# GpSimd makes the low half of a weight chunk in four instructions instead of one

## The chip, the cores and the metric

The kernel runs on one core of a Trainium2 chip. The metric is device time in microseconds (us) from the first to the last instruction of an execution and what lies around it, lower is better. A core has a matrix engine (TensorE, PE in the profile, with PEld for its weight loads), VectorE (DVE), ScalarE (ACT), GpSimd (POOL) and SyncE (SP), which here only issues transfers. Each engine works through its own queue in order; they wait for one another by semaphores.

## The reference

Two layers (gated linear attention; sparse attention with an indexer that picks the best keys), each with layer norm and a gated embedding, and then a second block with five groups of mixers. All of it is in float32, and most of the time goes into products of a 512-token activation with large weights:

```python
def gla_mixer(x, w_in, w_a2, b_a, gn_g, w_out):
    h = x @ w_in                                   # 1024 x 6160
    ...
    return (o.astype(x.dtype) * jax.nn.silu(z)) @ w_out
...
for i in range(DEPTH):
    ...                                            # y = gla_mixer(...) or dsa_mixer(...)
    x = layer_norm(ALPHA * x + y, ln_g[i], ln_b[i])
    x = x + (p[i] @ ple_w[i]) * jax.nn.sigmoid(x @ ple_gate_w[i])
```

The kernel makes such a product from three faster ones: a weight w is split into a rounded high half and the rest, `low = w - high`, the activation likewise, and high x high, high x low and low x high are added up in PSUM (`split_product`, L211).

## The kernel before, in words

Weights come in chunks of 256 columns by 1024 rows: on the chip a tile of 128 partitions x 8 k-tiles x 256 columns, 2048 float32 values a partition, 1 MB. Three rings of RING = 2 slots hold them: `w_ring` (as loaded), `w_high` and `w_low`. A chunk goes through four engines in order:

- `load_chunks` (SyncE): waits until the low half of the chunk that held the slot before is made (`w_low_made`), then issues the transfer into `w_ring`.
- `split_high` (ScalarE, L184): waits for the landing and for TensorE's release of the chunk two before, then copies `w_ring` to `w_high`, rounding it.
- `split_low` (GpSimd, L193): waits for `w_high_made` and subtracts: `w_low = w_ring - w_high`. It counts `w_low_made`.
- `chunk` (TensorE): waits for `w_low_made` and uses both halves, 48 or 96 matrix instructions over some 11 us. The matrix instructions of all products are recorded at L209.

The first chunk of all is split apart from this, in two halves (L451), and is not touched by the change. The very last one is 2 k-tiles of 1024 columns. Two chunks are narrow, 72 and 80 columns a k-tile. The two `mem_w_kv` chunks are not split and do not pass here.

Which phases the prediction speaks of:

- `phase_post`, once behind each layer: the output projection, then layer norm token tile by token tile. `layer_norm(j)` on VectorE is a chain of small steps around two instructions of 1024 columns, L1173 (inputs `x` and `gain`) and L1178 (inputs `x` and `shift`), with a square root on ScalarE between them (L1074, `rstd_x`). TensorE meanwhile multiplies an embedding (`w_ple`), waits for the first gate chunk, uses it for token tile 0, and then turns the `x` of token tile 2 (L879, waits for L1178).
- `phase_dsa`, the sparse attention: rotations on VectorE (L1547 to L1552), and from about 662 us the top-k search: L1602 and L1603 sixteen times over a tile, then L1604 (a subtraction with two inputs) and L1605 (a scalar operation).
- `phase_project`, the second block's projections: `norm_heads` on VectorE is L2002 and L2005 for each token tile, with two inputs in SBUF each; behind two of them stands L2022, which makes `a_tok`, for which TensorE waits.
- `phase_rwkv`, the last phase: chains of two-input instructions (L3172, L3174, L3175, `bt` at L3181), beside three GpSimd subtractions of the same kind at L3149 that the change leaves alone.

Of the kernel before, what the change touches and what calls it, by code (L numbers as in the profile page):

```python
# [7 lines left out]
F32 = mybir.dt.float32  # L8
# [16 lines left out]
RING = 2  # L25
# [51 lines left out]
class Program:  # L77
# [109 lines left out]
    def split_low(self, pool, upto=None):  # L187

        while self.lows < self.highs and (upto is None or self.splits[self.lows] < upto):
            i, n = self.lows, self.splits[self.lows]  # L190
            _, k, cols, _, _ = self.chunks[n]
            pool.wait_ge(self.w_high_made, i + 1)
            self.nc.gpsimd.tensor_tensor(self.slot(self.w_low, i % RING, k, cols), self.slot(self.w_ring, n % RING, k, cols),  # L193
                                         self.slot(self.w_high, i % RING, k, cols).bitcast(F32), ALU.subtract).then_inc(self.w_low_made, 1)
            self.lows += 1

    def chunk(self, pe, n):
# [3277 lines left out]
```

## Time and profile before

| | |
|---|---|
| median of 3 runs | 1610.26 us (1609.72 to 1610.45) |
| profiled execution | 1610.07 us, its span 1608.3 us |
| TensorE busy | 1510.5 us, 94% |
| VectorE busy | 678.1 us, 42% |
| ScalarE busy | 528.4 us, 33% |
| GpSimd busy | 549.9 us, 34%, 216 instructions |
| L193, GpSimd, all low halves | 414.1 us busy, 91 instructions, 803.4 us idle before them |
| mean granted TensorE clock | 0.971 |

Times in the rows are counted from the span's start. Busy time is the union of an engine's instructions. An instruction of VectorE or GpSimd that is issued and can't begin shows as a long one, so what looks like work may be waiting. A row of the timeline ends, in brackets, with the engine's idle time before it and what ended it. The granted clock is 1.00 at the higher of TensorE's two levels (2.4 GHz) and 0.50 at the lower (1.2 GHz).

### The profile page before, as it was taken

To read this page: it belongs to the slowest core of one execution; us is meant where nothing else is said; L and a number is where in the kernel's file an instruction comes from. 1 tells how busy PE (TensorE), PEld (TensorE's weight loads), DVE (VectorE), ACT (ScalarE), POOL (GpSimd) and SP (SyncE) were. 2 spreads that over 40 slices of the span, in tenths; PEclk is the share of its full clock that TensorE was granted. 3 is DMA by queue.
4 is the path that set the end of the run, shared out by engine and by line. 5 is a ranking of instruction groups with operands and counts; after the bars stand their busy time and mean duration, and the time that the engine had idled before them with its cause. 6 is when DMAs were issued, how large, how long until landed. Compare 5 with 4: busy or idle time off the path is not lost. (4 is left out here: it accounts for less than half of the span.)

```text
span 1608.3 us, 23500 instructions
## 1 busy us (share of the span) xinstructions
PE 1510.5 (94%) x9997; PEld 1312.5 (82%) x9997; DVE 678.1 (42%) x1356; ACT 528.4 (33%) x862; POOL 549.9 (34%) x216
## 2 busy tenths in 40 slices
PE   7999999999999999988999999999989997858998
PEld 7898875998997977766787899889879875748897
DVE  7032540222144273695545214441252135688424
ACT  3444225232223223333444222343342244421211
POOL 6333420333332248642643233224242411412121
PEclk9999999999999999998999999999999999978999
DMA  5223220223312332220111422243332200020111
GB/s 163 90 68 102 82 75 5 63 96 139 137 62 71 112 100 84 76 82 27 53 53 34 160 83 79 67 153 89 105 93 65 79 26 1 0 79 1 54 53 53
DMA packets 113751, 121.21 MB, mean 75 GB/s; under 512 B 12530, under 2 KB 107614, under 8 KB 113391
## 3 DMA queue, kind: packets, MB, share of 16 engines
q1 hardware_dynamic: 110096, 113.77, 22.2%
q10 hardware_dynamic: 3550, 5.94, 1.0%
q8 instruction: 79, 1.29, 0.3%
q14 instruction: 26, 0.21, 0.0%
HBM read 113.41 MB, written 6.29 MB: 74 GB/s over the span
## 5 line engine op out<-in xcount | busy, mean ns | idle before, releaser
L193 POOL TENSOR_TENSOR w_low<-w_ring,w_high 128x2048 fp32r<-128x2048 f32 (+1 forms) x91 | 414.1, 4550 | 803.4 <-ACT w_high L184 803.0
L209 PE MATMUL ps<-w_high,xT_high 128*128 128x256 f32 (+1 forms) x1056 | 305.1, 289 | 9.3 <-POOL w_low L451 4.4
L209 PE MATMUL ps<-w_high,xT_low 128*128 128x256 f32 (+1 forms) x1056 | 299.1, 283 | 0.0
L209 PE MATMUL ps<-w_low,xT_high 128*128 128x256 f32 (+1 forms) x1056 | 299.0, 283 | 0.0
L184 ACT ACTIVATE w_high<-w_ring 128x2048 fp32r<-128x2048 f32 (+1 forms) x91 | 171.5, 1885 | 316.5 <-PE ps L209 311.0
L209 PE MATMUL ps<-xT_high,w_high 128*128 128x512 f32 (+1 forms) x600 | 242.4, 404 | 2.8 <-POOL w_low L193 1.8
L209 PE MATMUL ps<-xT_high,w_low 128*128 128x512 f32 (+1 forms) x600 | 238.7, 398 | 0.0
L209 PE MATMUL ps<-xT_low,w_high 128*128 128x512 f32 (+1 forms) x600 | 237.6, 396 | 0.0
L209 PEld LDWEIGHTS ps<-w_high,xT_high 128*128 128x128 f32 x1056 | 202.8, 192 | 16.6 <-issue 6.4
L209 PEld LDWEIGHTS ps<-w_low,xT_high 128*128 128x128 f32 x1056 | 202.7, 192 | 1.7 <-issue 1.7
L209 PEld LDWEIGHTS ps<-w_high,xT_low 128*128 128x128 f32 x1056 | 202.3, 192 | 0.0
L209 PE MATMUL ps<-w_high,gT_high 128*128 128x256 f32 x512 | 146.2, 286 | 3.9 <-DVE gT_low L288 3.9
L209 PE MATMUL ps<-w_high,gT_low 128*128 128x256 f32 x512 | 145.6, 284 | 0.0
L209 PE MATMUL ps<-w_low,gT_high 128*128 128x256 f32 x512 | 145.5, 284 | 0.0
L209 PEld LDWEIGHTS ps<-xT_high,w_high 128*128 128x128 f32 (+1 forms) x600 | 112.9, 188 | 32.4 <-issue 2.9
L209 PEld LDWEIGHTS ps<-xT_high,w_low 128*128 128x128 f32 (+1 forms) x600 | 112.5, 188 | 28.4
L209 PEld LDWEIGHTS ps<-xT_low,w_high 128*128 128x128 f32 (+1 forms) x600 | 112.9, 188 | 26.3
L209 PEld LDWEIGHTS ps<-w_high,gT_high 128*128 128x128 f32 x512 | 99.0, 193 | 4.4 <-DVE gT_low L288 4.4
L209 PEld LDWEIGHTS ps<-w_low,gT_high 128*128 128x128 f32 x512 | 99.0, 193 | 0.0
L209 PEld LDWEIGHTS ps<-w_high,gT_low 128*128 128x128 f32 x512 | 98.9, 193 | 0.0
L209 PE MATMUL ps<-dsa_kT,mix_a 128*128 128x128 f32 (+3 forms) x128 | 42.8, 464 | 12.1 <-DVE peak L1615 12.1
L1155 DVE SCALAR_TENSOR_TENSOR x<-x,ps 128x512 f32<-128x512 f32 x16 | 10.9, 684 | 102.6 <-PE ps L209 102.6
(504 smaller groups left out, 2287.1 us busy)
## 6 DMA issues: line engine op xcount, KB each, us to landing
w_ring<-in_gla_w_in_dram SPq DMA_DIRECT2D x24, 1024.0 KB, 5.4
w_ring<-in_dsa_w_in_dram SPq DMA_DIRECT2D x19, 1024.0 KB, 5.1
w_ring<-in_w_in_dram SPq DMA_DIRECT2D x18, 1024.0 KB, 5.2
w_ring<-in_gla_w_out_dram SPq DMA_DIRECT2D x8, 1024.0 KB, 4.9
w_ring<-in_ple_gate_w_dram SPq DMA_DIRECT2D x8, 1024.0 KB, 5.1
w_ring<-in_dsa_w_out_dram SPq DMA_DIRECT2D x8, 1024.0 KB, 5.1
x_scratch<-x SPq DMA_DIRECT2D x4, 1024.0 KB, 6.3
w_ring<-in_w_out_dram SPq DMA_DIRECT2D x4, 768.0 KB, 4.8
```

The lines of the kernel that those rows point to most:

```text
L184: self.nc.scalar.activation(self.slot(self.w_high, i % RING, k, cols), self.slot(self.w_ring, n % RING, k, cols), ACT.Copy).then_inc(self. ...
L193: self.nc.gpsimd.tensor_tensor(self.slot(self.w_low, i % RING, k, cols), self.slot(self.w_ring, n % RING, k, cols), self.slot(self.w_high, ...
L209: return self.nc.tensor.matmul(out, lhs, rhs, start=first, stop=last, skip_group_check=not check)
L1155: nc.vector.scalar_tensor_tensor(out=r[:, j, cols], in0=x[:, j, cols], scalar=ALPHA, in1=ps[:, i, :], op0=ALU.mult, op1=ALU.add).then_inc( ...
```

## The change

`split_low` cuts the k-tiles of a chunk into steps of a quarter (2 of 8) and issues one subtraction for each. Only the last one counts the semaphore `w_low_made`. So who waits for a chunk still waits for all of it.

```diff
             pool.wait_ge(self.w_high_made, i + 1)
-            self.nc.gpsimd.tensor_tensor(self.slot(self.w_low, i % RING, k, cols), self.slot(self.w_ring, n % RING, k, cols),
-                                         self.slot(self.w_high, i % RING, k, cols).bitcast(F32), ALU.subtract).then_inc(self.w_low_made, 1)
+            low, whole, high = (self.slot(w, m % RING, k, cols) for w, m in ((self.w_low, i), (self.w_ring, n), (self.w_high, i)))
+            step = -(-k // 4)
+            for a in range(0, k, step):
+                part = slice(a, min(a + step, k))
+                ins = self.nc.gpsimd.tensor_tensor(low[:, part], whole[:, part], high[:, part].bitcast(F32), ALU.subtract)
+            ins.then_inc(self.w_low_made, 1)
             self.lows += 1
```

In GpSimd's queue before, from the first layer's chunks (24 in a row) over the norm stage (12, behind L1244) to the first rotated heads of the sparse attention:

```order
L862 UNCONDITIONAL_BRANCH
L193 TENSOR_TENSOR w_low<-w_ring,w_high 128x2048 x24
L1244 UNCONDITIONAL_BRANCH
L193 TENSOR_TENSOR w_low<-w_ring,w_high 128x2048 x12
L1664 UNCONDITIONAL_BRANCH
L193 TENSOR_TENSOR w_low<-w_ring,w_high 128x2048
L193 TENSOR_TENSOR w_low<-w_ring,w_high 128x8x72
L193 TENSOR_TENSOR w_low<-w_ring,w_high 128x2048 x2
L1667 TENSOR_TENSOR mix_a<-mix_a,head_cos 32x512
```

The same place of the changed kernel, whose lines stand four further down:

```order
L866 UNCONDITIONAL_BRANCH
L197 TENSOR_TENSOR w_low<-w_ring,w_high 128x512 x96
L1248 UNCONDITIONAL_BRANCH
L197 TENSOR_TENSOR w_low<-w_ring,w_high 128x512 x48
L1668 UNCONDITIONAL_BRANCH
L197 TENSOR_TENSOR w_low<-w_ring,w_high 128x512 x4
L197 TENSOR_TENSOR w_low<-w_ring,w_high 128x2x72 x4
L197 TENSOR_TENSOR w_low<-w_ring,w_high 128x512 x8
L1671 TENSOR_TENSOR mix_a<-mix_a,head_cos 32x512
```

Nothing changes its place; each instruction of a chunk has become four, and the queues of the other engines hold what they held.

## Rows read from the trace of the kernel before

**Rows 1.** Waits of TensorE: who waited for whom, us in total, times, longest:

```profile
PE ps L209 <- DVE peak L1615: 12.1, 4, 11.1
...
PE ps L209 <- POOL w_low L193: 5.2, 3, 1.8
...
PE ps L1867 <- DVE a_tok L2022: 4.7, 1, 4.7
...
PE ps L879 <- DVE x L1178: 3.8, 2, 1.9
```

**Rows 2.** GpSimd by shape: count, busy us, mean ns, idle before:

```profile
L193 POOL TENSOR_TENSOR w_low<-w_ring,w_high 128x2048 fp32r<-128x2048 f32 x89 | 411.1, 4619 | 792.6 <-ACT w_high L184 792.1 <-POOL level L465 0.3
```

**Rows 3.** Timeline (start, us, engine, line), GpSimd behind a low half:

```profile
613.28 1.29 POOL L1667 TENSOR_TENSOR mix_a<-mix_a,head_cos 32x512 f32<-32x512 f32 x1
...
614.53 1.29 POOL L1668 TENSOR_TENSOR rot<-rot,head_sin 32x512 f32<-32x512 f32 x1
```

**Rows 4.** Timeline of GpSimd, then of VectorE, last phase:

```profile
1452.26 3.81 POOL L3149 TENSOR_TENSOR mix_low<-mixT,mix_high 128x1536 fp32r<-128x1536 f32 x1 [20.11 <-DVE branch_room L3175]
...
1456.02 3.88 POOL L3149 TENSOR_TENSOR mix_low<-mixT,mix_high 128x1536 fp32r<-128x1536 f32 x1
...
1459.86 2.81 POOL L3149 TENSOR_TENSOR mix_low<-mixT,mix_high 128x1024 fp32r<-128x1024 f32 x1
...
1452.69 3.91 DVE L3181 TENSOR_TENSOR bt<-LT,levelT 128x512 f32<-128x512 f32 x1
```

**Rows 5.** Timeline of GpSimd, first layer-norm stage:

```profile
475.43 4.52 POOL L193 TENSOR_TENSOR w_low<-w_ring,w_high 128x2048 fp32r<-128x2048 f32 x1 [16.89 <-ACT w_high L184]
```

**Rows 6.** Timeline of VectorE, first layer-norm stage:

```profile
476.06 4.98 DVE L1173 SCALAR_TENSOR_TENSOR x<-x,moments,gain 128x1024 f32<-128x1024 f32 x1
...
481.14 5.42 DVE L1178 SCALAR_TENSOR_TENSOR x<-x,rstd_x,shift 128x1024 f32<-128x1024 f32 x1
```

**Rows 7.** Timeline of ScalarE, first layer-norm stage:

```profile
478.85 0.19 ACT L1074 ACTIVATE rstd_x<-rstd_x 128x1 f32<-128x1 f32 x1
```

**Rows 8.** Timeline of TensorE, first layer-norm stage:

```profile
480.00 0.38 PE L209 MATMUL ps<-w_high,xT_high 128*128 128x256 f32 x1 [1.68 <-POOL w_low L193]
...
486.70 0.30 PE L879 MATMUL ps<-ident,x 128*128 128x128 f32 x1 [1.90 <-DVE x L1178]
```

**Rows 9.** Stretches of TensorE: length, busy (instructions), granted clock, DMA share, GB/s:

```profile
480.80:484.10 3.30, 3.30 (x23) 1.00 0.88 287
593.40:596.70 3.30, 3.30 (x10) 0.50 0.93 310
1204.40:1211.10 6.70, 5.40 (x26) 0.50 0.47 153
```

**Rows 10.** Timeline of GpSimd, then VectorE, then TensorE, chunk at 587:

```profile
587.41 4.75 POOL L193 TENSOR_TENSOR w_low<-w_ring,w_high 128x2048 fp32r<-128x2048 f32 x1 [11.01 <-ACT w_high L184]
...
587.76 4.94 DVE L1552 TENSOR_TENSOR prob<-prob,dsa_gated 128x512 f32<-128x512 f32 x1
...
592.21 0.50 PE L209 MATMUL ps<-xT_high,w_high 128*128 128x512 f32 x1 [1.83 <-POOL w_low L193]
```

**Rows 11.** Timeline of GpSimd, then VectorE, top-k search:

```profile
674.81 4.64 POOL L193 TENSOR_TENSOR w_low<-w_ring,w_high 128x2048 fp32r<-128x2048 f32 x1 [2.71 <-ACT w_high L184]
...
678.39 1.35 DVE L1604 TENSOR_TENSOR left<-left,prob 128x256 f32<-128x256 f32 x1
...
679.77 0.29 DVE L1605 TENSOR_SCALAR left<-left 128x256 f32<-128x256 f32 x1
```

**Rows 12.** Timeline of GpSimd, then VectorE, head norms:

```profile
1198.55 4.57 POOL L193 TENSOR_TENSOR w_low<-w_ring,w_high 128x2048 fp32r<-128x2048 f32 x1 [6.56 <-ACT w_high L184]
...
1199.71 4.49 DVE L2002 TENSOR_TENSOR heads<-heads,head_ss 128x1024 f32<-128x1024 f32 x1
...
1205.47 0.17 DVE L2022 TENSOR_TENSOR a_tok<-gates,cum 128x16 f32<-128x16 f32 x1
```

**Rows 13.** Timeline of VectorE, last phase:

```profile
1429.88 2.81 DVE L3172 TENSOR_TENSOR branch_room<-LT,levelT 128x512 f32<-128x512 f32 x1
```

## The prediction

> **What bounds the kernel now.** I read the page's busy shares first: TensorE works 94% of the span, GpSimd 34%, so GpSimd as such is no bound. Then TensorE's waits [rows 1]: of its idle time only 5.2 us, in three pieces, ends with a low half made at L193. All other chunks are ready before TensorE asks for them. But the same list names waits on VectorE that belong to this change: two on `x` (L1178, 3.8 us), one on `a_tok` (L2022, 4.7 us) and an 11.1 us one on `peak` (L1615) behind VectorE's top-k search. In the timeline some VectorE instructions with two SBUF inputs last exactly until a GpSimd instruction ends and then their own length: 4.98 us for x at L1173 [rows 6], whose 1024 columns take the 1.08 us that are left behind the low half's end at 479.95 [rows 5, 6]. So VectorE and GpSimd exclude each other there, instruction by instruction. The change cuts the piece that VectorE waits for; it also lets VectorE in between the pieces of a chunk that TensorE waits for.
>
> **One chunk by itself.** A low half of 2048 columns takes 4.62 us (89 of them) [rows 2]. A GpSimd two-input instruction of 512 columns takes 1.29 us, and the next starts 1.25 us after it [rows 3]. Four of them: 3 x 1.25 + 1.29 = 5.04, that is +0.43 us a chunk. Bounds: +0.54 if nothing overlaps (4 x 1.29 - 4.62), +0.1 if the pieces lose nothing but their own start, from rows 4: of the low halves at L3149 the first ends 3.28 us after the port was given back (1452.78 to 1456.06) with 1536 columns, the last 2.22 us after it (1460.45 to 1462.67) with 1024, so 2.07 ns a column and 0.10 us fixed; 4 x (0.10 + 1.06) = 4.64. I take 0.43, the row of the same length. In all, 90 chunks become four instructions and one becomes two. 91 x 0.43 = 39 us more of GpSimd, nearly all beside TensorE's work: rows 1 have three waits on L193 and no more; by the timeline a steady chunk is used 3.6 us or more after its end, and the tightest that don't wait have 0.9 and 1.7 us. In the attention layer GpSimd also has the rotations of the heads in its queue and is busy from 608.7 to 646 without a pause, so four chunks' additions pile up there to 1.7 us; its chunks have over 6 us to spare in that stretch. SyncE's next load waits for the last piece too, 0.43 us later, which ScalarE hides by waiting for TensorE's release anyway.
>
> The Trainium skill ("GPSIMD Engine Reference", section 3.1) gives 2.6 cycles an element at 1.2 GHz and 4497 ns for 2048 columns; that leaves some 60 ns of fixed cost, and by that estimate four pieces would cost +0.18 us a chunk. The row of 512 columns speaks for more; the sum would be 0.8 us smaller by the page.
>
> **Who gets in between.** Three GpSimd instructions stand back to back with VectorE's bt (L3181) queued [rows 4]: the first GpSimd one ends at 1456.06, the second is issued at 1456.02, and yet VectorE's ends at 1456.61 (1452.69 + 3.91, the chain's 4.44 us for two) and the second GpSimd one at 1459.90, late by VectorE's 0.55 us. They take turns. So with four pieces, a two-input VectorE instruction waits for at most one piece, and each one that comes costs the chunk its own length. A piece right behind VectorE takes 0.10 + 1.06 = 1.16 us.
>
> The Trainium skill ("SBUF — State Buffer", section "SBUF: two separate sides") says that the pair of ports is an exclusive lock held for the whole instruction. The trace agrees (4.98 us for x). By that rule alone the cut would only help VectorE; what it does to the chunk is the turns of rows 4.
>
> **The two layer-norm stages** (475 and 996, alike to 0.02 us). Now: low half 475.43 to 479.95, TensorE waits 1.68 until 480.00 [rows 5, 8]; x of L1178 is held by the next low half until 486.56, TensorE waits 1.90 until 486.70. After: piece 1 ends 476.72; L1173 (asked at 476.06) runs to 477.80; piece 2 to 478.96; piece 3 to about 480.20, since L1178 needs ScalarE's rstd_x, made 479.04 [rows 7], and comes too late for that turn; L1178 runs to 481.28; piece 4 to 482.44. TensorE starts at 482.48, not 480.00: +2.48. From there its next 4.80 us of work (480.00 to 484.80) are as before, so it comes to x at 487.2 and x has long been there: the 1.90 goes. Net +2.48 - 1.90 = +0.6, less some 0.1 of overlap: **+0.5 each, +1.0**. Bounds for one: 0.2 (pieces at their cheapest) to 0.9.
>
> Two waits of under 2 us become one of 1.68 + 2.48 = 4.16 us. The granted clock [rows 9] is 1.00 after the idle 1.68 (480.8 to 484.1) but 0.50, the lower level of 1.2 GHz, after the idle 1.83 at 592.21 and for 6.7 us after the idle 4.71 at 1205.70. So I expect a stretch at the lower level in both stages. Work in it takes twice its time: 3.3 us busy in the row at 593.4 is a loss of 1.65, 5.4 us at 1204.4 a loss of 2.7; part of the stretch can fall into the wait itself. I take 1.5 each, **+3.0**; bounds 0 and 2.7 each.
>
> **Chunk at 587.41** [rows 10]. One VectorE instruction (L1552, 0.55 us net) is in it. Pieces: 588.70; L1552 to 589.25; 590.41; 591.65; 592.90. TensorE starts 592.95 instead of 592.21: **+0.7**, and the clock has fallen there already. Bounds 0.3 to 1.0.
>
> **Top-k search.** VectorE is the bound from 661.7 to 728.8. There L1604 waits for a low half (1.35 us instead of the 0.4 that 256 columns take) [rows 11]. With pieces: low half from 674.81, the third ends 678.60, L1604 runs to 678.88; the fourth, waiting, takes its turn until 680.04; L1605, in SBUF on both sides too, waits for it and ends about 680.2 instead of 680.06. The stall has moved by one instruction. A second round, at 700, goes alike. **+0.2** for both; if L1605 doesn't need the port, -1.9.
>
> **Head norms** [rows 12]. L2002, L2005 and L2022 follow one another on VectorE and TensorE waits for a_tok. Now: the low half ends 1203.12, L2002 1204.20, L2005 (1024 columns too) some 1.1 later, a_tok 1205.64. After: piece 1 ends 1199.84, L2002 1200.92, piece 2 1202.08, L2005 1203.16, piece 3 1204.32, a_tok 1204.36: TensorE starts at 1204.4, not 1205.70, **-1.3**, with the last piece behind it where nobody waits (that chunk has 14 us to spare). The idle time falls from 4.71 to 3.4, so I take the shorter of the stretches at the lower level for the longer one, 2.7 - 1.65, **-1.0**. Bounds -2.6 and -0.9 together.
>
> **Last phase.** At 1429.88 L3172 waits 2.1 us for a low half [rows 13] on the chain that ends last, but L3174 and L3175, with two SBUF inputs each, come right behind it and let the remaining pieces in. They end where they did, **+0.1**. The other stalls of VectorE (v_tok at L856, gate at L1221, the rotations before 587) end before anyone waits for them.
>
> Sum: 1.0 + 3.0 + 0.7 + 0.2 - 2.3 + 0.1 = **+2.7 us** on the profiled execution's 1610.07 (span 1608.3 and 1.8 around it), which is 0.19 under the median of 1610.26: **1612.8 us**. A measurement of this kernel can tell about 0.2%, 3.2 us, from no change.
>
> **The rivals.**
> - *The clock costs more.* If the three stretches are as long as the one at 1204.4 and the head norms keep theirs: 2 x (0.9 + 2.7) + 1.0 + 0.4 - 1.3 + 0.1 = +7.4, 1617.5. For it: an idle 4.71 did this once. Against: that stretch held transposes and a part of the wait.
> - *The clock stays up* in both norm stages, as it did after 1.68 and 1.90: -3.0, so -0.3, 1609.8.
> - *Faster: VectorE's release doesn't delay the chunk.* If VectorE's instructions slip in where GpSimd pauses anyway (0.10 us between pieces and more at its dispatch), low half 32 ends at 480.5, x is ready in time and the waits of 1.90 and 1.86 go without a new one: 2 x (0.5 - 1.9) = -2.8; with +0.3 at 587, -1.9 in the top-k search and -2.3 at the head norms -6.7, 1603.4. It decides once a queued piece of GpSimd no longer starts late by VectorE's length; rows 4 speak against it, for two-input instructions of both.
> - *No turns between pieces:* GpSimd's queue keeps the port for all four. Then every stall lengthens by 0.43 and nothing is won: 2 x 0.43 (norms) + 0.3 + 0.86 + 0.43 + 0.43 = +2.9, 1613.0. The same time by another way; rows 4 speak against it, but those are three instructions of one loop with other operands.
>
> **How the numbers follow.** My forecast 0.46, its own range 1610.5 to 1615. Clock costs more 0.17; clock stays up 0.17; no turns 0.10; faster 0.10. The range leaves out the faster rival's outer part and the far end of the costly one: 1608 to 1616.5. Slower by over 0.2% (over 1613.5): 0.16 of my case (its upper third), 0.16 of the costly clock, 0.03 of no turns, 0.35. Faster: 0.07 of the faster rival and 0.02 of the rest, 0.09. Within 0.2%: 0.56.
>
> **What would show it.** Rows of w_low at 1.2 to 1.3 us, four in 5.0 us where VectorE is quiet. In both norm stages TensorE waits for w_low about 4.2 us, once, and not for x; VectorE's L1173 lasts 1.7 instead of 4.98. After it a stretch of 0.50 in the granted clock. The wait on a_tok near 3.4 us. L1604 short and L1605 long. The forecast is wrong if the wait for w_low stays under 2.5 us, if VectorE's stalls still last as long as a whole chunk, or if TensorE waits for w_low in the steady stretches.

## The result and the profile after

The changed kernel takes 1615.27 us (median of 14 runs, 1613.14 to 1617.67), the kernel before beside it 1610.39 (14 runs, 1608.79 to 1614.16). The ratio is 1.0029, 95% interval [1.0022, 1.0036], or +4.7 us with [3.5, 5.8]. So it is slower by 0.29%, a little over what a measurement can tell. I had said +2.7. Lines behind the edit are 4 higher than before (L193 is now L197, L209 L213, L1173 L1177, L1178 L1182, L2022 L2026).

The profiled execution took 1615.83 us, span 1614.1, 5.8 more than the one before. 1.4 of these came before 392 us, ahead of all that is explained here; e5, which cuts nothing before 1189 us, is already 1.7 later than the kernel before at the first layer-norm stage. So the profile serves for the mechanism and the medians for the sizes. Its list of TensorE's waits, which answers to [rows 1] (who waited for whom: us, times, longest):

```profile
PE ps L213 <- DVE peak L1619: 12.3, 4, 11.2
PE ps L213 <- POOL w_low L197: 10.8, 3, 4.1
...
PE ps L1871 <- DVE a_tok L2026: 1.8, 1, 1.8
```

The wait on `x` is gone from the list, that on `w_low` has gone from 5.2 to 10.8 us, still in three pieces, and the one on `peak` has stayed. The low halves by shape, which answers to [rows 2], and two neighbouring pieces of a quiet chunk from the timeline of GpSimd:

```profile
L197 POOL TENSOR_TENSOR w_low<-w_ring,w_high 128x512 fp32r<-128x512 f32 x352 | 459.0, 1335 | 737.0 <-ACT w_high L184 736.6 <-POOL level L469 0.3
```

```profile
62.34 1.29 POOL L197 TENSOR_TENSOR w_low<-w_ring,w_high 128x512 fp32r<-128x512 f32 x1 [11.49 <-ACT w_high L184]
63.59 1.29 POOL L197 TENSOR_TENSOR w_low<-w_ring,w_high 128x512 fp32r<-128x512 f32 x1
...
66.08 1.29 POOL L197 TENSOR_TENSOR w_low<-w_ring,w_high 128x512 fp32r<-128x512 f32 x1
```

The quiet chunk lasts from 62.34 to 67.37, 5.03 us, where the same chunk took 4.61 before and [rows 2] have 4.62 on average. The mean of all pieces, 1335 ns, is longer than 1.29 since VectorE gets in between some of them. The first layer-norm stage shows it, GpSimd first (it answers to [rows 5]; x2 is two pieces in one row), then VectorE [rows 6], ScalarE [rows 7] and TensorE [rows 8]:

```profile
476.85 1.28 POOL L197 TENSOR_TENSOR w_low<-w_ring,w_high 128x512 fp32r<-128x512 f32 x1 [16.47 <-ACT w_high L184]
478.08 3.48 POOL L197 TENSOR_TENSOR w_low<-w_ring,w_high 128x512 fp32r<-128x512 f32 x2
481.52 2.25 POOL L197 TENSOR_TENSOR w_low<-w_ring,w_high 128x512 fp32r<-128x512 f32 x1
```

```profile
477.47 1.74 DVE L1177 SCALAR_TENSOR_TENSOR x<-x,moments,gain 128x1024 f32<-128x1024 f32 x1
480.50 0.16 DVE L1179 RECIPROCAL rstd_x<-rstd_x 128x1 f32<-128x1 f32 x1 [1.30 <-ACT rstd_x L1078]
480.70 1.94 DVE L1182 SCALAR_TENSOR_TENSOR x<-x,rstd_x,shift 128x1024 f32<-128x1024 f32 x1
```

```profile
480.28 0.19 ACT L1078 ACTIVATE rstd_x<-rstd_x 128x1 f32<-128x1 f32 x1
```

```profile
483.82 0.58 PE L213 MATMUL ps<-w_high,xT_high 128*128 128x256 f32 x1 [4.07 <-POOL w_low L197]
484.20 0.42 PE L213 MATMUL ps<-w_low,xT_high 128*128 128x256 f32 x1
...
484.84 0.42 PE L213 MATMUL ps<-w_low,xT_high 128*128 128x256 f32 x1
...
490.99 1.04 PE L883 MATMUL ps<-ident,x 128*128 128x128 f32 x8
```

Piece 1 ends at 478.13 and L1177 right behind it lasts 1.74 us instead of 4.98. Its 1.1 us make piece 2 late, piece 3 is quiet, L1182 makes piece 4 late (2.25 us where a quiet one has 1.28). The chunk takes 6.92 us from 476.85 to 483.77, 4.52 before. TensorE waits 4.07 instead of 1.68, and its transposes of `x` at 490.99 wait for nothing. But from 483.82 to 490.99 are 7.17 us; the same work took 486.70 - 480.00 - 1.90 = 4.80 before [rows 8]. That is the clock. Two rows of the kernel before to set beside 484.20 and 484.84, three matrix instructions apart as those are:

```profile
480.22 0.28 PE L209 MATMUL ps<-w_low,xT_high 128*128 128x256 f32 x1
...
480.57 0.28 PE L209 MATMUL ps<-w_low,xT_high 128*128 128x256 f32 x1
```

Three instructions took 0.35 us there and 0.64 in the changed kernel, 1.8 times as long. Stretches of TensorE (from:to, length, busy (instructions), granted clock, DMA share, GB/s), which answer to [rows 9]:

```profile
482.60:489.40 6.80, 5.58 (x25) 0.50 0.45 154
1008.30:1011.70 3.40, 3.21 (x15) 0.50 0.61 184
...
1206.20:1209.70 3.50, 3.50 (x19) 0.51 0.00 0
```

The first stage lost 2.39 - 1.90 + 2.37 = 2.9 us. By the shift of TensorE's rows (how much later than before the same instruction starts, ahead of the wait and behind the stage) it is 2.8. The second stage, alike but with the shorter stretch, lost 1.7 by that shift: 5.26 us later ahead of its wait, 7.00 behind it.

The chunk that was at 587 [rows 10], the two instructions of the top-k search [rows 11], and the head norms [rows 12] (GpSimd, VectorE, TensorE):

```profile
597.24 0.50 PE L213 MATMUL ps<-xT_high,w_high 128*128 128x512 f32 x1 [2.70 <-POOL w_low L197]
...
1212.12 0.60 PE L1871 MATMUL ps<-ident,a_tok 128*4 128x128 f32 x4 [1.81 <-DVE a_tok L2026]
```

```profile
683.43 0.52 DVE L1608 TENSOR_TENSOR left<-left,prob 128x256 f32<-128x256 f32 x1
683.98 1.27 DVE L1609 TENSOR_SCALAR left<-left 128x256 f32<-128x256 f32 x1
...
1206.79 1.90 DVE L2006 TENSOR_TENSOR heads<-heads,head_ss 128x1024 f32<-128x1024 f32 x1
1208.61 2.30 DVE L2009 TENSOR_TENSOR heads<-heads,gains 128x1024 f32<-128x1024 f32 x1
...
1211.05 1.01 DVE L2026 TENSOR_TENSOR a_tok<-gates,cum 128x16 f32<-128x16 f32 x1
```

```profile
1206.33 1.28 POOL L197 TENSOR_TENSOR w_low<-w_ring,w_high 128x512 fp32r<-128x512 f32 x1 [5.16 <-ACT w_high L184]
1207.57 2.27 POOL L197 TENSOR_TENSOR w_low<-w_ring,w_high 128x512 fp32r<-128x512 f32 x1
1209.80 2.24 POOL L197 TENSOR_TENSOR w_low<-w_ring,w_high 128x512 fp32r<-128x512 f32 x1
1212.00 1.27 POOL L197 TENSOR_TENSOR w_low<-w_ring,w_high 128x512 fp32r<-128x512 f32 x1
```

The stall has moved from L1608 (0.52 us, 1.35 before) to L1609 (1.27, 0.29 before). At the head norms each of VectorE's three instructions waits for one piece, and a_tok comes sooner. TensorE's wait for it reads 1.81 here and not the 3.34 of e1 and e3 to e6, because TensorE itself was late: its work ahead of the wait ran at the lower level (1206.2 to 1209.7).

### The profile page after: what moved, and what is told of

Read it like the earlier page. It is cut to its first block and busy times, and to the rows that moved or that the text cites. A ratio compares the mean times of both kernels' runs of the same rounds, so it can differ in the third digit from the quotient of the medians.

```text
span 1614.1 us, 23771 instructions
## 1 busy us (share of the span) xinstructions
PE 1516.1 (94%) x9997; PEld 1319.5 (82%) x9997; DVE 644.8 (40%) x1356; ACT 527.7 (33%) x862; POOL 604.7 (37%) x487
## 3 DMA queue, kind: packets, MB, share of 16 engines
q8 instruction: 79, 1.29, 0.3%
## 5 line engine op out<-in xcount | busy, mean ns | idle before, releaser
L197 POOL TENSOR_TENSOR w_low<-w_ring,w_high 128x512 fp32r<-128x512 f32 (+2 forms) x362 | 469.1, 1327 | 756.9 <-ACT w_high L184 756.4
L213 PE MATMUL ps<-w_high,xT_high 128*128 128x256 f32 (+1 forms) x1056 | 307.8, 291 | 13.9 <-POOL w_low L197 8.1
L213 PE MATMUL ps<-w_low,xT_high 128*128 128x256 f32 (+1 forms) x1056 | 302.0, 286 | 0.0
L213 PE MATMUL ps<-w_high,xT_low 128*128 128x256 f32 (+1 forms) x1056 | 301.8, 286 | 0.0
L213 PE MATMUL ps<-xT_high,w_high 128*128 128x512 f32 (+1 forms) x600 | 242.3, 404 | 3.7 <-POOL w_low L197 2.7
L213 PE MATMUL ps<-xT_high,w_low 128*128 128x512 f32 (+1 forms) x600 | 239.0, 398 | 0.0
L213 PE MATMUL ps<-xT_low,w_high 128*128 128x512 f32 (+1 forms) x600 | 237.8, 396 | 0.0
L213 PEld LDWEIGHTS ps<-w_high,xT_high 128*128 128x128 f32 x1056 | 205.3, 194 | 20.9 <-POOL w_low L197 9.8
L213 PEld LDWEIGHTS ps<-w_low,xT_high 128*128 128x128 f32 x1056 | 205.5, 195 | 1.7 <-issue 1.7
L213 PEld LDWEIGHTS ps<-w_high,xT_low 128*128 128x128 f32 x1056 | 205.2, 194 | 0.0
L213 PE MATMUL ps<-w_high,gT_high 128*128 128x256 f32 x512 | 146.5, 286 | 3.9 <-DVE gT_low L292 3.9
L213 PE MATMUL ps<-w_high,gT_low 128*128 128x256 f32 x512 | 145.8, 285 | 0.0
L213 PE MATMUL ps<-w_low,gT_high 128*128 128x256 f32 x512 | 145.8, 285 | 0.0
L213 PEld LDWEIGHTS ps<-xT_high,w_high 128*128 128x128 f32 (+1 forms) x600 | 112.7, 188 | 33.3 <-POOL w_low L197 3.2
L213 PEld LDWEIGHTS ps<-xT_high,w_low 128*128 128x128 f32 (+1 forms) x600 | 112.8, 188 | 28.0
L213 PEld LDWEIGHTS ps<-xT_low,w_high 128*128 128x128 f32 (+1 forms) x600 | 113.0, 188 | 26.6
L213 PEld LDWEIGHTS ps<-w_high,gT_high 128*128 128x128 f32 x512 | 99.1, 193 | 4.4 <-DVE gT_low L292 4.4
L213 PEld LDWEIGHTS ps<-w_low,gT_high 128*128 128x128 f32 x512 | 99.2, 194 | 0.0
L213 PEld LDWEIGHTS ps<-w_high,gT_low 128*128 128x128 f32 x512 | 99.1, 194 | 0.0
L213 PE MATMUL ps<-dsa_kT,mix_a 128*128 128x128 f32 (+3 forms) x128 | 42.9, 464 | 12.3 <-DVE peak L1619 12.3
L1680 POOL TENSOR_TENSOR gT_low<-dsa_gated,gT_high 128x512 fp32r<-128x512 f32 x16 | 20.6, 1287 | 85.9 <-ACT gT_high L1514 85.9
```

The lines of the kernel that those rows point to most:

```text
L197: ins = self.nc.gpsimd.tensor_tensor(low[:, part], whole[:, part], high[:, part].bitcast(F32), ALU.subtract)
L213: return self.nc.tensor.matmul(out, lhs, rhs, start=first, stop=last, skip_group_check=not check)
L1680: nc.gpsimd.tensor_tensor(gT[1][:, h, :], gated[:, h % 2, :], gT[0][:, h, :].bitcast(F32), ALU.subtract).then_inc(sem["head_low"], add("he ...
```

## The experiments

The theory: the change costs time in the two layer-norm stages, through VectorE's turns between the pieces and through the clock that falls in the longer wait; it gives some back at the head norms; the other longer chunks cost nothing. The rivals: the longer chunks as such (GpSimd 55 us busier), or a chunk elsewhere that TensorE now waits for. The kernel before was measured again beside each group of four, so its median is 1610.01 for e1 to e4, 1610.35 for e5 to e8 and 1610.96 for e9 to e12. Differences below are the recorded ratio minus 1, times the median of before beside it, with the 95% interval. That ratio is not the quotient of the two medians: in e1 the medians lie 1.6 us apart and the ratio gives 0.5. The edits are shown against the changed kernel, where nothing else is said. One execution of e1 (2157 us) and one of e4 (6593 us) lie far from all others and are left out of the medians and ratios here; nothing explains them. `i` is the number of the chunk: 32, 33 and 64, 65 are the first two of the layer-norm stages, 40 the one at 587, 47 and 49 stand in the top-k search, 79, 80 at the head norms.

**e1: the layer-norm stages as before, all else in four pieces.**

```
-            step = -(-k // 4)
+            step = k if i in (32, 33, 64, 65) else -(-k // 4)
```

> Four pieces for all chunks but the four of the two layer-norm stages (chunks 32, 33, 64 and 65), which stay whole. My theory (VectorE gets turns between the pieces, the chunk comes 2.4 us later, TensorE's one long wait costs the clock): the stages lose nothing, so the time is that of the changed kernel less 2.8 and 1.7 us, about 1610.8, level with the kernel before; TensorE's waits there are 1.7 on w_low and 1.9 on x as before. Rival (the 39 us more of GpSimd work or the longer chunks everywhere are what costs): still 3 us or more slower than before, about 1614.

Measured 1611.60 against 1610.01: +0.5 us [-1.0, +2.1], where 1610.8 was expected. The waits of 1.68 on w_low and 1.86 on x are back. So most of the 4.7 us sits in four chunks of 91.

**e2: the layer-norm stages alone in four pieces.**

```
+            step = -(-k // 4) if i in (32, 33, 64, 65) else k
```

> Only the four chunks of the two layer-norm stages are made in four pieces, all others whole. My theory: all of the loss of these stages and none of the gain at the head norms: +4.5 to +5 us over the kernel before, about 1615; one wait of 4.1 us on w_low in each stage, none on x, and a stretch at the lower clock behind it. Rival (the loss lies in the other chunks): within 1 us of the kernel before.

Measured 1614.62: +4.8 us [3.4, 6.4]. TensorE's first wait, and the stretches behind both, in the trace of e2:

```profile
483.25 0.58 PE L213 MATMUL ps<-w_high,xT_high 128*128 128x256 f32 x1 [4.07 <-POOL w_low L197]
```

```profile
481.30:488.10 6.80, 4.85 (x22) 0.50 0.47 154
1003.60:1010.40 6.80, 5.39 (x25) 0.50 0.47 155
```

The waits alone make 2 x (4.07 - 1.68) - 1.90 - 1.86 = +1.0 us, so the clock cost 3.8. The traces agree: by the shift of TensorE's rows the two stages lost 2.5 and 2.7 us in this execution, 2.8 and 1.7 in that of the whole change. Their mean is 2.4 a stage, and half of the 4.8 is 2.4.

**e3: the wait filled.** The whole change, and two groups of products (1.7 us each by the wait, 4.07 - 0.66 for both) into a PSUM bank that the gate products overwrite right behind, put into TensorE's wait for the low half:

```
+                pe.wait_ge(sem["y_added"], past["y_added"] + NT + 1)
+                for _ in range(2):
+                    embed(NT, 0, 0)
```

> The changed kernel, and in each layer-norm stage TensorE does four more matrix instructions (two embeddings of 512 columns, 3.8 us, into a PSUM bank that is overwritten next) while it waits for the chunk. If the part of the loss beyond the later chunk is the clock (my theory): no stretch at 0.50 behind the two waits, and 1.5 to 2 us less in each stage, about 1612. Rival (the loss is only the later chunk and later work in the queue): the same time as the changed kernel, 1615, or more.

Measured 1611.32 against 1610.01: +0.6 us [-1.1, +2.3], so 4.1 us less than the change without it (some 2 us to either side, the two intervals combined), although TensorE does more. In its trace the wait reads 0.66 and TensorE works through both stages at the upper level:

```profile
482.57 0.38 PE L213 MATMUL ps<-w_high,xT_high 128*128 128x256 f32 x1 [0.66 <-POOL w_low L197]
482.79 0.28 PE L213 MATMUL ps<-w_low,xT_high 128*128 128x256 f32 x1
```

```profile
482.60:489.40 6.80, 6.80 (x40) 1.00 0.45 154
1004.50:1011.30 6.80, 6.80 (x40) 1.00 0.48 155
```

The low half is as late as in the changed kernel: it starts at 475.59 and TensorE gets it at 482.57, 6.98 us later (476.85 and 483.82 there, 6.97). Only the clock behind the wait differs, and it is worth about 4 us in both stages together, most of the loss. This is not a finding of one trace: the mean granted clock was recorded for every execution. It is 0.965 to 0.970 in the 14 of the changed kernel (0.967 on average) and in the 10 of e2 (0.968). In the 11 of e3 it is 0.967 to 0.974, 0.971 on average, and so it is in the 33 of the kernel before beside them.

**e4: VectorE made to come behind the chunk.** The whole change, but in the stages L1177 of token tile 2 waits for the low half, so that no turn of VectorE falls into it:

```
+                    if j == 2:
+                        dve.wait_ge(g.w_low_made, g.chunks[gates][3] + 1)
```

> The changed kernel, but in each layer-norm stage VectorE's first long instruction on token tile 2 waits until the whole low half of the first gate chunk is made, so it takes no turn between its pieces. My theory (turns): the chunk takes 5.0 us instead of 6.9 and TensorE waits 2.1 to 2.3 us for it, without a wait on x, since the next chunk's pieces let VectorE in; 4 us less in each stage than the changed kernel, about 1607 to 1608, below the kernel before. Rival (the pieces are slow by themselves, whoever runs beside them): the chunk still takes over 6 us and the time stays at 1615 or rises.

In the trace it did what it should: L1179 (that was L1177) comes at 481.32, and the wait is 2.10, that is 0.42 above the 1.68 of before, the bare price of the pieces.

```profile
481.34 0.39 PE L213 MATMUL ps<-w_high,xT_high 128*128 128x256 f32 x1 [2.10 <-POOL w_low L197]
```

```profile
481.32 1.28 DVE L1179 SCALAR_TENSOR_TENSOR x<-x,moments,gain 128x1024 f32<-128x1024 f32 x1 [4.27 <-POOL w_low L197]
```

The turns are shown by this: without them the chunk is 1.97 us sooner (4.07 to 2.10). But the time missed its expectation of 1607 to 1608: 1610.22, +0.2 us [-1.6, +1.9], where the waits make 2 x 0.42 - 3.76 = -2.9. In the profiled execution (1607.63) no stretch at the lower level stood behind either wait, and by the shift of TensorE's rows each stage gained 1.7 us: the low half comes 0.42 later, and the missing wait on x gives back 2.1, 0.2 more than it reads. The runs spread from 1606.28 to 1613.06. The slower ones have the lower clock: 0.966 on average in the five over 1611 us, 0.969 in the six under it. The open question was whether a wait of 2.1 us brings the clock down in the others.

**e9: e4 with its wait filled** by one such group.

```
+                pe.wait_ge(sem["y_added"], past["y_added"] + NT + 1)
+                embed(NT, 0, 0)
```

> This is e4 (VectorE's multiply of x comes behind the low half, in both layer-norm stages) plus one product group into a bank that is written anew behind it, 1.9 us of TensorE work, put into TensorE's wait for the low half of 2.1 us. It asks why e4, whose profiled span was 8 us shorter than the changed kernel's, came out at 1610.97 by its median. Theory 'clock': in other executions of e4 the wait of 2.1 us brought the lower level of the clock on; with the wait filled that cannot happen, and the time is 1606 to 1607.5, with no stretch of 0.50 at 482 and at 1007. Rival 'not the clock': 1610 to 1611.5, as e4. If the filling work ends later than the low half it adds up to 0.3 us a stage.

Measured 1607.81 against 1610.96: -2.9 us [-4.5, -1.4], 3.1 less than e4 (some 2.3 to either side), though the low half comes at the same time in both. That is 0.3 above the range of the theory "clock" (1606 to 1607.5) and well under that of its rival (1610 to 1611.5). The mean granted clock goes the same way, 0.9692 in the 11 executions against 0.9675 in the 11 of e4. But where it fell in e4's other executions was not seen: only one trace was kept, and that one has a mean clock of 0.968 with no stretch behind the waits. So a cost of the clock behind a wait of 2.1 us is likely and not shown.

**e11: the control, the kernel before with half a group in its wait of 1.68**, which then reads 0.83.

```
+                pe.wait_ge(sem["y_added"], past["y_added"] + NT + 1)
+                g.product(ps[:, NT, :], pT[:, 0, 0:P], w_ple[:, 0, 0:COLS])
```

> The kernel before with the same 0.94 us of TensorE work in the two waits of 1.68 us. It is the control for the filled kernels: if filling wins something by itself, 1608 to 1609; if waits of this length cost the clock nothing, the time of the kernel before within 0.5 us.

Measured 1611.19: +0.3 us [-1.1, +1.8]. Filling wins nothing by itself. It wins where the wait is long: 4 us at 4.07, about 3 at 2.10 (less sure), nothing that could be told at 1.68.

**e5: the head norms alone.**

```
+            step = -(-k // 4) if i in (79, 80) else k
```

> Only chunks 79 and 80, the two beside VectorE's head norms, are made in four pieces. My theory: a_tok is ready 1.3 us earlier relative to the chunk before it, TensorE's wait for it falls from 4.7 to 3.4 us, and part of the stretch at the lower clock goes with it: 1.3 to 3.8 us under the kernel before, about 1607.5. Rival (VectorE's stalls are no loss, since other waits end at the same time): no difference.

Measured 1609.83 against 1610.35: -1.1 us [-2.4, +0.2], short of the 1.3 to 3.8 expected and not clear of nothing. TensorE's wait for a_tok, and the stretch behind it:

```profile
1206.36 0.98 PE L1871 MATMUL ps<-ident,a_tok 128*4 128x128 f32 x4 [3.34 <-DVE a_tok L2026]
```

```profile
1206.40:1209.80 3.40, 3.40 (x17) 0.50 0.31 66
```

4.71 - 3.34 = 1.37 us less of waiting, and the stretch at the lower level has 3.40 us of work where [rows 9] have 5.40. By the shift of TensorE's rows the two together gave 2.3 us in this trace, so the clock 0.9. The median gives 1.1 for both; the interval reaches to the -2.3 of the trace.

**e8: all chunks in four pieces but those of the stages, 587, the top-k search and the head norms.**

```
+            step = k if i in (32, 33, 40, 47, 49, 64, 65, 79, 80) else -(-k // 4)
```

> Four pieces for every chunk except the nine beside the layer norms, the rotations, the top-k search and the head norms (32, 33, 40, 47, 49, 64, 65, 79, 80), which stay whole. My theory: 82 chunks at 0.43 us, 35 us more of GpSimd work, cost nothing: within 0.6 us of the kernel before. Rival (the longer chunks cost somewhere that I did not see): 1.5 us or more slower.

Measured 1609.87 against 1610.35: -0.6 us [-2.1, +0.6]. Eighty-two chunks that last 0.4 us longer cost nothing. The rival "longer chunks as such" is out.

**e7: halves for quarters**, everywhere.

```
-            step = -(-k // 4)
+            step = -(-k // 2)
```

> All chunks in two halves instead of four pieces. My theory (turns): in the layer-norm stages only one turn of VectorE comes into the first chunk, and L1182 gets its port after the second half at the latest: the chunk takes about 5.9 us, TensorE waits 3.0 us for it and not for x; between the kernel before and the changed one, about 1612 to 1614. Rival (the cost goes with the number of pieces, 0.43 us at four and a third of it at two): 1611 or less.

Measured 1613.04 against 1610.35: +2.1 us [0.5, 3.7]. The waits are 2.81 and 2.79, a_tok's 4.68 as before the change, and each stage has one short stretch at the lower level:

```profile
483.00:486.40 3.40, 3.40 (x18) 0.51 0.68 224
1005.10:1008.60 3.50, 3.50 (x19) 0.53 0.67 234
```

Waits: 2 x (2.80 - 1.68) - 3.76 = -1.5, and +0.6 at 587 (2.42 for 1.83). By the shift of TensorE's rows each stage lost 0.6 us, its short stretch included, so the sum with 587 is +1.7.

**e12: only the second chunk of each stage in four pieces.** It is the one that VectorE's L1178 waits for, and TensorE doesn't wait for it:

```
+            step = -(-k // 4) if i in (33, 65) else k
```

> Four pieces only for the second chunk of each layer-norm stage (i = 33 and 65). The wait of 1.68 us for the first low half stays, the wait for x (1.90 and 1.86 us) goes: -3.8 by the waits alone, -4 to -5 with what e6 gained over it (6.3, of which the head norms gave 1.1 alone): 1605.2 to 1606.5. Rival: e6's gain came from the head norms together with the stages and not from the stages alone: 1608 or more.

Measured 1605.34 against 1610.96: ratio 0.9967 [0.9955, 0.9979], -5.3 us [-7.2, -3.4]. In the timeline of its GpSimd and VectorE the first low half is whole and holds L1177 for 4.98 us as before; in the second L1182 gets its turn behind one piece:

```profile
482.45 5.97 POOL L197 TENSOR_TENSOR w_low<-w_ring,w_high 128x512 fp32r<-128x512 f32 x4 [0.98 <-ACT w_high L184]
```

```profile
477.57 4.98 DVE L1177 SCALAR_TENSOR_TENSOR x<-x,moments,gain 128x1024 f32<-128x1024 f32 x1
...
482.66 2.15 DVE L1182 SCALAR_TENSOR_TENSOR x<-x,rstd_x,shift 128x1024 f32<-128x1024 f32 x1
```

**e6: e12 and the head norms.**

```
+            step = -(-k // 4) if i in (33, 65, 79, 80) else k
```

> Four pieces only for chunks 33, 65, 79 and 80. In the layer-norm stages the chunk that TensorE waits for (32, 64) stays whole, and the one behind it, which holds VectorE's second long instruction, is cut. My theory (a cut pays where VectorE waits and nobody waits for the chunk): TensorE's wait on w_low stays 1.7, the wait of 1.9 on x goes in both stages, and the head norms gain as in the run with those two alone: 3.8 us from the waits and 1.3 to 3.8 at the heads, 1603 to 1605, the fastest of all. Rival (cutting costs the chunks a turn each time, and the clock takes the gain): within 1 us of the kernel before.

Measured 1604.45 (5 runs) against 1610.35: ratio 0.9961 [0.9948, 0.9974], -6.3 us [-8.4, -4.2]. The waits on w_low are 1.68 twice and that on x is gone:

```profile
PE ps L213 <- POOL w_low L197: 5.2, 3, 1.8
...
PE ps L1871 <- DVE a_tok L2026: 3.3, 1, 3.3
```

**e10: e6 with the half group of e11 in its wait of 1.68.**

> This is e6 (four pieces only for the second chunk of each layer-norm stage and the two at the head norms; 1604.45 us in its runs) plus 0.94 us of TensorE work in the wait of 1.68 us for the first low half of each stage. Theory: that wait holds the clock at its upper level in the profile of e6, so there is nothing left for the filling to win: 1604 to 1605, ratio 0.996. Rival 'the wait of 1.68 costs the clock in some executions': 1602 to 1603.5.

Measured 1604.12 against 1610.96: -5.6 us [-7.6, -3.5]. That is from 5 runs. The filling adds nothing to e6 that could be told, as in e11. e6, e10 and e12 beat both kernels; among themselves the intervals don't tell them apart, and e12 is the smallest edit.

## Why the prediction was right in its steps and short in two terms

| term | predicted | measured | by |
|---|---|---|---|
| norm stages, the waits | +1.0 | +1.0 | 4.07 once for 1.68 and 1.90 |
| norm stages, the clock | +3.0 | +3.8 | e2 less its waits (4.1 by e3) |
| chunk at 587 | +0.7 | +0.9 | 2.70 for 1.83 |
| top-k search | +0.2 | +0.1 | wait on peak 11.2 for 11.1 |
| head norms, wait and clock | -2.3 | -1.1 | e5 |
| all other chunks, last phase | +0.1 | 0 | e8, -0.6 [-2.1, +0.6] |
| sum | +2.7 | +4.7 | ratio of the whole change, +4.7 |

The split of the stages' 4.8 us into 1.0 and 3.8 goes by the waits as they read; with the 2.1 us that the missing wait on `x` is worth by the shift of TensorE's rows (e4, e12) it is 0.6 and 4.2.

The intervals of e2 and e5 reach 1.3 to 1.6 us to either side, so that the sum of the parts meets the whole to 0.1 is partly luck. The measured 1615.27 us lies in the range of 1608 to 1616.5 but 0.3 above that of my own case (1610.5 to 1615), and of the three outcomes it is the one with 0.35, slower by over 0.2%, and not the one with 0.56. Two terms were mis-sized: the clock in the stages by 0.8 us, the head norms by 1.2.

*The turns.* Right. The prediction let L1173 in behind piece 1, L1178 behind piece 3, and had the wait at 4.16 us; it is 4.07 in both stages. A piece behind VectorE lasts 2.25 us by its row, of which 1.1 are VectorE's, so 1.16 of its own, as worked out from [rows 4]. e4 takes the turns away and the wait falls to 2.10. The two rivals that hung on this are out: in "faster" the low half would not have been late, in "no turns" L1173 would still have lasted 5 us. The Trainium skill ("SBUF — State Buffer", section "SBUF: two separate sides") has whoever starts first hold the pair of ports for the whole instruction. The trace agrees, and for L1609 too: it has one SBUF input, writes SBUF, and waited in L1608's place.

*The price of a cut.* Right: four pieces took 5.03 us where the same chunk took 4.61, +0.42, and 4.95 where it took 4.52 (e4, first stage), +0.43; I had 0.43. The lower bound beside it was misadded: 4.64 us is 0.02 above the 4.62 of [rows 2], and the +0.1 holds only against a quick chunk of 4.52. Nothing hung on it. The Trainium skill's figures ("GPSIMD Engine Reference", section 3.1) had given +0.18 by my estimate. For 2048 columns the trace is near it, 4.52 to 4.62 us where the page has 4497 ns. For the pieces it doesn't agree: they start 1.25 us apart, not at a quarter of the page's time; the measurement decides.

*The clock in the stages.* The mechanism was right (e3: fill the wait and 4 us come back), the size was not: I took 1.5 a stage and it is 1.9 to 2.0. I had two rows, a short stretch (loss 1.65) and a long one (2.7), and took a little less than the short one because part of a stretch can fall into the wait. The traces show both: long and short in the change (5.58 and 3.21 us of work), long twice in e2, short twice in e7, whose wait is 2.8. Of the four stretches behind a wait of 4.07, three were long: this is what the 1.5 had wrong. A second step erred the other way: "Work in it takes twice its time". The rows have 1.8 times (0.64 us for 0.35), so 5.58 us of work lose 2.5 us and not 2.8, and 3.3 us lose 1.5 and not 1.65. The shift of TensorE's rows bears this out: take a stage's loss, less the longer wait, plus the 2.1 us that the missing wait on `x` gives (e12), and the stretches cost 2.5 and 1.4 us in the change, 2.2 and 2.4 in e2 and 1.5 twice in e7. The four behind a wait of 4.07 have a mean of 2.1, where 1.9 to 2.0 was measured. The rival "the clock costs more" had the long stretch right and its price of 2.7 too high; "the clock stays up" is out.

*The head norms.* The wait fell by 1.37 (-1.3 predicted) and the trace of e5 shows the short stretch for the long one, as the step said, but the time shows only 1.1 us for both. In the execution of the changed kernel and in those of e9, e10, e11 and e12 a stretch at the lower level also lay ahead of the wait, where it costs nothing, since VectorE's chain ends it. Where such a stretch lies differs from one execution to the next, so a saving in the clock read from one trace is not one in the median. The interval of e5 does not exclude the -2.3. This term stays the least certain.

## What to carry to other kernels

A long GpSimd instruction on the port that VectorE needs can be cut so that VectorE gets in after one piece; then every VectorE instruction that does get in delays GpSimd's result by its own length. So cut only the chunks whose result nobody waits for while VectorE is held, here two of 91 (e12, -5.3 us), and leave those that TensorE waits for whole (the cut of all gave +4.7). When waits are added up, a wait twice as long is not worth twice as much: two of 1.7 and 1.9 us cost themselves alone, one of 4.1 cost itself and 2 us of clock behind it. Where such a long wait can't be shortened, filling it with products that nobody reads gave the clock's part back here.

## What the runs showed of the hardware that was not expected

- Useless work made the kernel faster: 6.8 us of products added in two waits of 4.07 us took about 4 us off the time (e3), 3.4 us in two waits of 2.10 about 3 (e4 to e9, less sure), 1.7 us in two of 1.68 nothing that could be told (e11, e10).
- Executions of the same kernel differ by up to 6 us (before: 1607.40 to 1613.30 in 26 runs), as much as everything in question here, and the profiled ones differ in where the granted clock is at its lower level. The trace of e6 was its fastest execution (1600.03 for a median of 1604.45), that of e10 its slowest (1607.89 for 1604.12); by their spans alone e10 would have looked 8 us worse.
- e12 and e6 gained 1.4 to 1.5 us more than -3.8 (the waits) and -4.9 (the waits and e5's 1.1). Their intervals hold the smaller figures. By the shift of TensorE's rows each stage of e12 gained 2.1 us where the wait was 1.90 or 1.86, which is 0.4 of it. In the traces of e12 and e6 the stretch at the lower level behind the chunk at 587 [rows 9] is missing too, and TensorE's rows are 1.5 us earlier behind that place. But it is also missing in the trace of e2, which is no faster for it, and it is there in that of e10. So whether a gain is left is open.
